# The scaling of attention's probabilities moves from GpSimd into VectorE's order

## The chip, the cores and the metric

One core of one Trainium2 chip runs the whole program, one launch of a hand-scheduled kernel: every engine has its own instruction stream, and semaphores order them. The metric is the device time of one launch in microseconds (us), the median of several runs; lower is better.

## The reference

One step of a hybrid decoder layer over 1024 prompt tokens and 8 sample tokens, all in fp32. What matters here is the prompt's attention: 8 query heads of width 64 in two groups of four (two key heads), each query block of 128 tokens attending in three branches, whose results are weighted by a gate and added:

```
s_c = einsum('nthgd,nbhd->nthgb', q, kv_cmp[:, :, 0]) * scale
p_c = masked_softmax(s_c, ...)                 # compressed: 16 blocks of keys
p_s = masked_softmax(s_s, ...)                 # selected: all keys up to the query's block
p_w = masked_softmax(s_w, w_mask)              # window of 512 keys
return gates[..., 0:1] * o_c + gates[..., 1:2] * o_s + gates[..., 2:3] * o_w
```

`masked_softmax` subtracts the row's maximum, takes the exponential and divides by the row's sum. Since the three weighted outputs are added, the kernel multiplies each head's exponentials by gate / sum (the **share**) and then adds all three products in one accumulator. Beside attention the layer has a projection of the merge gates, `h @ w_in[:, 1816:]`, 2048 columns, which doesn't depend on attention.

## The kernel before, in words

fp32 products of full accuracy are made of single-pass ones: an operand is cut into a high part (a copy rounded to the fp32r type) and a low part (the difference), and hi*hi, hi*lo and lo*hi are added.

**The attention stage** (lines 1007 to 1375) has 32 **units** (`units`, L1009), in the order i (query block, 0 to 7), kv (key head, 0 and 1), branch: first the window branch, which takes the compressed one with it (in the text "window unit"), then the selected branch ("selected unit"). A unit holds four heads, and so two **pairs**. A unit's keys are cut in **blocks** of 128 (`key_blocks`, L1018): i+1 blocks in a selected unit; min(i, 4)+1 and one of 16 compressed keys in a window unit. There are 148 blocks (`blocks`, L1027).

While the blocks of unit n are worked off, the four heads of unit n+1 are prepared: `jobs_at(t)` (L1031) says at which block t of unit n the scores of head k of unit n+1 are made. For a unit of six blocks these are blocks 0, 1, 2, 3; for units of up to three blocks all four fall on the first block.

What each engine does, in its own fixed order:

- **PE (TensorE)**, L1194 to L1204, for each block t: `scores` of the jobs (into one of two PSUM buffers; waits `exp_done` of the job two before, L1146), `turn` (L1160: four transposes of the scaled probabilities, 128 keys of four heads, into a ring of two PSUM tiles; at a unit's first block it waits until the unit's probabilities are scaled, L1165 to L1170), and `values` of the block before (L1177: products with the value rows; waits for the low part, `plo_ready`). Between these stand **fills**: steps of the merge gates' projection (`fill`, L1110; 192 steps of six products, spread over the blocks by L1046 to L1064).
- **ACT (ScalarE)**, L1249 to L1273: `exps` (exponential with bias and row sum, L1208), `cut` (the high part of a turned block, L1229), `gate` (a finished gate chunk out of PSUM, L1247), `cut_gate_hi` (the high part of the next gate weights, L918, at fixed places, L1271).
- **DVE (VectorE)**, L1354 to L1375, for each block t: `maxima` of the jobs (L1303), `cut` (the low part of the turned block, L1336), then `shares` (L1315) of a pair whose second head is done: reciprocal of the sums (L1325) times the gates (L1326). The shares of a job of block t-1 stand behind the cut of block t; those of the last block stand behind that same block's cut (L1367 to L1370). `cut_q` (L1339) and `take` (L1347) come in once per query block and once per key head.
- **POOL (GpSimd)**, L1280 to L1297: for each unit and pair, it waits for the pair's share and multiplies the exponentials of both heads, in place, by their shares (`tensor_scalar`, L1290): in a window unit 16 compressed and up to 640 window columns per head, in a selected unit (i+1)*128. For i of 5 and more, DVE takes the first head of a selected pair itself (`dve_heads`, L1014; L1327 to L1330). After the pairs of unit n come the low parts of the gate weights (`cut_gate_lo`, L920 to L923) that belong to the blocks of unit n-1. The PE's first fill on a set of gate weights waits for that low part (L1115). Fourteen of the sixteen sets are cut in this stage.
- **SP** writes the gate chunks to DRAM and loads the next gate weights (L1098 to L1106).

The stage ends with a barrier; the decode stage behind it begins with loads that SP issues after the barrier.

Of the kernel before, what the change touches and what calls it, by code (L numbers as in the profile page):

```python
# [18 lines left out]
ALU = mybir.AluOpType  # L19
AX = mybir.AxisListType  # L20

P = 128
# [11 lines left out]
WB = WINDOW // P  # L34
# [4 lines left out]
NCB = TP // BLOCK  # L39
# [37 lines left out]
class Buffers:  # L77
# [12 lines left out]
    def at(self, name, shape, dt, offset):  # L90
        size = 2 if dt == BF16 else 4
        for n in shape[1:]:
            size *= n
        assert self.base + offset + size <= self.end, (name, self.base + offset + size - self.end)
        return self.nc.alloc_sbuf_tensor_at(name, shape, dt, offset=self.base + offset), offset + (size + 31) // 32 * 32
# [148 lines left out]
def hybrid_step(nc, x_prompt, x_sample, cache_cmp_kv, cache_sel_kv, state_win_kv, state_pool, page_table,  # L244
# [3 lines left out]
    with ExitStack() as root:  # L248
        sem = Semaphores(nc)
# [34 lines left out]
        with ExitStack() as st:  # L284
# [28 lines left out]
            with nc.Block() as block:  # L313

                @block.sync
                def _(sp):
                    sp.dma_start(crow[0:1, :], c_prompt).then_inc(c_loaded, 16)
                    sp.dma_start(crow[1:1 + NS, :], c_sample).then_inc(c_loaded, 16)
                    for at_row, v in ((VB_ADA, b_ada), (VG_PRE_MIX, g_pre_mix), (VG_POST_MIX, g_post_mix),
                                      (VG_PRE_MLP, g_pre_mlp), (VG_POST_MLP, g_post_mlp), (V_POOL, pool_scale)):  # L320
                        v = v[0].rearrange("(r p) -> r p", p=P)
                        sp.dma_start(vrow[at_row:at_row + v.shape[0], :], v).then_inc(vec_loaded, 16)
                    for c in range(NA):
                        if c >= NR:
                            sp.wait_ge(ada_done, c - NR + 1)
                        sp.dma_start(wa[:, c % NR], columns_of(w_ada[0], c * AC, AC)).then_inc(wa_loaded[c % NR], 16)
                    in_load(sp)
# [170 lines left out]
        with ExitStack() as st:  # L498
            accs = [psum(st, f"in_acc{s}", [P, NCH, 512]) for s in range(2)]
            g = gin  # L500
# [161 lines left out]
        def rows_of(kv):  # L662
            return slice(kv * HD, (kv + 1) * HD)
# [232 lines left out]
        NGT = 2 * KD  # L896
# [23 lines left out]
        def cut_gate_lo(pool, u):  # L920

            pool.wait_ge(gw_hi_ready, u + 1)
            pool.tensor_tensor(gw_lo[:, u % 2], gw_raw[:, u % 2], gw_hi[:, u % 2].bitcast(F32), ALU.subtract).then_inc(gw_lo_ready, 1)  # L923
# [83 lines left out]
        SEL, WIN, CMP = 0, TP, TP + WINDOW + P  # L1007
        NKP = CMP + NCB + 2
        units = [(i, kv, br) for i in range(NB) for kv in range(KVH) for br in range(2)]  # L1009
        NUN = len(units)  # L1010
        PAIRS = GRP // 2
        RING = 2

        def dve_heads(i):  # L1014

            return 1 if i >= 5 else 0

        def key_blocks(n):  # L1018

            i, _, sel = units[n]  # L1020
            if sel:
                return [(0, b, SEL + b * P, P) for b in range(i + 1)]
            first = max(0, i - WB)
            return [(1, b, WIN + (b - first) * P, P) for b in range(first, i + 1)] + [(2, 0, CMP, NCB)]

        blocks_before = [sum(len(key_blocks(m)) for m in range(n)) for n in range(NUN + 1)]
        blocks = [(n, z) for n in range(NUN) for z in range(len(key_blocks(n)))]  # L1027
        NBL = len(blocks)
# [8 lines left out]
        def last_block(t):  # L1037

            return t + 1 == blocks_before[blocks[t][0] + 1]

        def by_dve_before(n):

            return sum(PAIRS for m in range(n) if units[m][2] and dve_heads(units[m][0]))


        NSTEP = 4 * NGU  # L1046
        FIRST = 8
# [18 lines left out]
        def gate_cuts_at(t):  # L1066

            return [x // 12 + 1 for x in steps_at[t] if x % 12 == 5 and 2 <= x // 12 + 1 < NGT]

        with ExitStack() as st:  # L1070
            at = buf.slabs(3)
            prob = at("prob", [P, GRP, NKP])
# [10 lines left out]
            share = buf.const("share", [P, 2, GRP, 3])  # L1083
# [2 lines left out]
            out = psum(st, "attn_out", [P, 512])  # L1086
            gps = psum(st, "gate_ps", [P, 512])
            qhi_ready, qlo_ready, scores_done, bias_ready, exp_done = (sem(n) for n in ("qhi_ready", "qlo_ready", "scores_done", "bias_ready", "exp_done"))
            share_ready, win_scaled, rest_scaled, sel_scaled, pT_done, phi_ready, plo_ready, pv_done, out_taken = (
                sem(n) for n in ("share_ready", "win_scaled", "rest_scaled", "sel_scaled", "pT_done", "phi_ready", "plo_ready", "pv_done", "out_taken"))  # L1090
            half_ready, zeroed_q = sem("out_half_ready"), sem("q_lo_zeroed")
            achain = sem("dve_chain3")

# [1 line left out]
            with nc.Block() as block:  # L1095
# [13 lines left out]
                def _(pe):  # L1109
# [50 lines left out]
                    def turn(t):  # L1160

                        n, z = blocks[t]
                        i, _, sel = units[n]
                        _, _, c, m = key_blocks(n)[z]
                        if z == 0 and not sel:  # L1165
                            pe.wait_ge(win_scaled, (n // 2 + 1) * PAIRS)
                        elif z == 0:
                            pe.wait_ge(rest_scaled, (n // 2 + 1) * PAIRS)
                            if dve_heads(i):
                                pe.wait_ge(sel_scaled, by_dve_before(n + 1))  # L1170
                        if t >= RING:
                            pe.wait_ge(plo_ready, t - RING + 1)
                        for g in range(GRP):
                            last = pe.transpose(pT[t % RING][0:m, g * P:(g + 1) * P], prob[:, g, c:c + m], ident[:])  # L1174
                        last.then_inc(pT_done, 1)
# [99 lines left out]
                @block.gpsimd  # L1275
                def _(pool):
                    for kv in range(KVH):
                        last = pool.memset(ql[rows_of(1 - kv), kv].bitcast(F32), 0.0)
                    last.then_inc(zeroed_q, 1)
                    for n in range(NUN):  # L1280
                        i, _, sel = units[n]
                        nw = (min(i, WB) + 1) * P
                        for pair in range(PAIRS):
                            pool.wait_ge(share_ready, n * PAIRS + pair + 1)
                            todo = [(1, SEL, (i + 1) * P)] if sel else [(2, WIN, nw), (0, CMP, NCB)]
                            own = dve_heads(i) if sel else 0
                            for g in range(2 * pair + own, 2 * pair + 2):
                                for which, c, m in todo:
                                    y = prob[:, g, c:c + m]
                                    last = pool.tensor_scalar(y, y, share[:, n // 2 % 2, g, which:which + 1], None, ALU.mult)  # L1290
                            last.then_inc(rest_scaled if sel else win_scaled, 1)
                        for t in range(blocks_before[n - 1] if n else 0, blocks_before[n] if n else 0):
                            for u in gate_cuts_at(t):
                                cut_gate_lo(pool, u)
                    for t in range(blocks_before[NUN - 1], NBL):
                        for u in gate_cuts_at(t):
                            cut_gate_lo(pool, u)  # L1297

                @block.vector
                def _(dve):  # L1300
# [14 lines left out]
                    def shares(n, pair):  # L1315

                        i, kv, sel = units[n]
                        dve.wait_ge(exp_done, n * GRP + 2 * pair + 2)
                        g0 = 2 * pair
                        g = slice(g0, g0 + 2)  # L1320
                        which = slice(1, 2) if sel else slice(0, 3, 2)
                        par = n // 2 % 2
                        x = share[:, par, g, which]
                        gates = gtok[:, i].rearrange("p (k g b) -> p k g b", k=KVH, g=GRP)[:, kv, g, which]
                        chain.then_wait(dve.reciprocal(x, total[:, par, g, which]))  # L1325
                        dve.tensor_tensor(x, x, gates, ALU.mult).then_inc(share_ready, 1)  # L1326
                        if sel and dve_heads(i):  # L1327
                            dve.wait_ge(share_ready, n * PAIRS + pair + 1)
                            y = prob[:, g0, SEL:SEL + (i + 1) * P]
                            dve.tensor_scalar(y, y, share[:, par, g0, 1:2], None, ALU.mult).then_inc(sel_scaled, 1)  # L1330

                    def cut(t):
                        n, z = blocks[t]
# [22 lines left out]
                    for k in range(GRP):  # L1356
                        maxima(0, k)
                        if k == 3:
                            shares(0, 0)
                    shares(0, 1)  # L1360
                    for t in range(NBL):
                        for n, k in jobs_at(t):
# [8 lines left out]
                        for n, k in jobs_at(t):  # L1371
                            i, kv, sel = units[n]
# [174 lines left out]
        with ExitStack() as st:  # L1547
            accs = [psum(st, f"merge_acc{s}", [P, NCH, 512]) for s in range(2)]
            g = gm
# [986 lines left out]
```

## Time and profile before

| | us |
|---|---|
| median of 3 runs | 1989.32 (1988.67 to 1989.78) |
| the profiled execution | 1988.15 |
| its span, first to last instruction | 1986.4 |
| the attention stage in it | about 416 to 934 |
| PE busy, share of the span | 89% |
| DVE, ACT, POOL busy, share of the span | 33%, 30%, 33% |

The profile is of one execution. Times in it are counted from the span's start; the 1.75 us between span and device time lie around the span. An engine's busy time is the sum of its instructions' durations; "idle before" is the time in which an engine stood still ahead of an instruction, with the work whose end released it. [...] In a row of the windows view, the busy times stand in the order PE, PEld (weight loads), DVE, ACT, POOL.

### The profile page before, as it was taken

To read this page: it belongs to the slowest core of one execution; us is meant where nothing else is said; L and a number is where in the kernel's file an instruction comes from. 1 tells how busy PE (TensorE), PEld (TensorE's weight loads), DVE (VectorE), ACT (ScalarE), POOL (GpSimd) and SP (SyncE) were. 2 spreads that over 40 slices of the span, in tenths; PEclk is the share of its full clock that TensorE was granted. 3 is DMA by queue.
4 is the path that set the end of the run, shared out by engine and by line. 5 is a ranking of instruction groups with operands and counts; after the bars stand their busy time and mean duration, and the time that the engine had idled before them with its cause. 6 is when DMAs were issued, how large, how long until landed. Compare 5 with 4: busy or idle time off the path is not lost. (4 is left out here: it accounts for less than half of the span.)

```text
span 1986.4 us, 26123 instructions
## 1 busy us (share of the span) xinstructions
PE 1773.0 (89%) x10956; PEld 1639.5 (83%) x10956; DVE 649.6 (33%) x1174; ACT 593.7 (30%) x1083; POOL 647.8 (33%) x451
## 2 busy tenths in 40 slices
PE   6899976668889888897699989899999999999997
PEld 2799965557777777775599989899999999999996
DVE  2411114243445554553144546310121121012135
ACT  3322211034445554553043435320121022002311
POOL 1454531024445553542013456222122112212421
PEclk9899996879999998998699999999999999999998
DMA  8343415301110100001264213211111111111411
GB/s 277 85 126 97 128 49 165 90 25 43 47 36 29 36 26 22 26 22 49 62 196 133 64 43 108 54 54 43 48 49 44 43 54 44 43 46 50 128 62 57
DMA packets 215048, 139.28 MB, mean 70 GB/s; under 512 B 53397, under 2 KB 211265, under 8 KB 214889
## 3 DMA queue, kind: packets, MB, share of 16 engines
q1 hardware_dynamic: 200171, 124.14, 21.8%
q10 hardware_dynamic: 14758, 13.44, 2.1%
q8 instruction: 89, 1.46, 0.3%
q14 instruction: 30, 0.25, 0.0%
HBM read 117.95 MB, written 21.92 MB: 70 GB/s over the span
## 5 line engine op out<-in xcount | busy, mean ns | idle before, releaser
L2032 POOL TENSOR_TENSOR ff_lo<-ff_raw,ff_hi 128x1024 fp32r<-128x1024 f32 x56 | 137.0, 2449 | 485.5 <-ACT ff_hi L1848 485.5
L1290 POOL TENSOR_SCALAR prob<-prob,share 128x16 f32<-128x16 f32 (+8 forms) x180 | 199.0, 1124 | 267.8 <-DVE share L1326 267.7
L1120 PE MATMUL gate_ps<-h_hi,gate_w_hi 128*128 128x344 f32 x384 | 142.9, 372 | 15.5 <-ACT gate_sum L1247 8.2
L2209 PE MATMUL ff_acc<-h_hi,ff_hi 128*128 128x344 f32 x672 | 142.6, 321 | 0.6 <-DVE relu_c L2358 0.6
L2209 PE MATMUL ff_acc<-h_lo,ff_hi 128*128 128x344 f32 x672 | 142.6, 320 | 0.0
L1336 DVE TENSOR_TENSOR p_lo<-pT,p_hi 128x512 fp32r<-128x512 f32 (+1 forms) x148 | 101.9, 688 | 122.6 <-ACT p_hi L1229 121.7
L2209 PE MATMUL ff_acc<-h_hi,ff_lo 128*128 128x344 f32 x672 | 141.9, 319 | 0.0
L1229 ACT ACTIVATE p_hi<-pT 128x512 fp32r<-128x512 f32 (+1 forms) x148 | 88.3, 597 | 164.8 <-PE pT L1174 164.3
L172 POOL TENSOR_TENSOR w_lo<-w_raw,w_hi 128x512 fp32r<-128x512 f32 (+1 forms) x31 | 56.3, 1820 | 233.1 <-ACT w_hi L168 143.8
L1218 ACT ACTIVATE prob<-scores,bias 128x640 f32<-128x640 f32 (+7 forms) x192 | 105.8, 557 | 78.8 <-DVE bias L1312 47.4
L1120 PE MATMUL gate_ps<-h_lo,gate_w_hi 128*128 128x344 f32 x384 | 127.0, 331 | 0.0
L1120 PE MATMUL gate_ps<-h_hi,gate_w_lo 128*128 128x344 f32 x384 | 126.8, 330 | 0.0
L2209 PE MATMUL ff_acc<-f_lo,ff_hi 128*128 128x344 f32 x576 | 122.2, 320 | 3.7 <-issue 3.7
L1848 ACT ACTIVATE ff_hi<-ff_raw 128x1024 fp32r<-128x1024 f32 x56 | 58.6, 1051 | 222.4 <-DMA ff_raw<-in_w_ff_dram 222.4
L2209 PE MATMUL ff_acc<-f_hi,ff_hi 128*128 128x344 f32 x576 | 122.4, 321 | 2.2 <-issue 2.2
L1174 PE MATMUL pT<-ident,prob 128*128 128x128 f32 (+1 forms) x592 | 95.8, 286 | 31.1 <-POOL prob L1290 30.9
L2209 PE MATMUL ff_acc<-f_hi,ff_lo 128*128 128x344 f32 x576 | 121.6, 319 | 0.0
L2209 PEld LDWEIGHTS ff_acc<-h_lo,ff_hi 128*128 128x128 f32 x672 | 113.7, 189 | 0.0
L2209 PEld LDWEIGHTS ff_acc<-h_hi,ff_hi 128*128 128x128 f32 x672 | 113.1, 188 | 0.8 <-issue 0.8
L2209 PEld LDWEIGHTS ff_acc<-h_hi,ff_lo 128*128 128x128 f32 x672 | 111.9, 188 | 0.0
L1174 PEld LDWEIGHTS pT<-ident,prob 128*128 128x128 f32 (+1 forms) x592 | 68.5, 141 | 49.6 <-POOL prob L1290 34.1
L1863 ACT ACTIVATE fraw<-relu 128x1032 f32<-128x1032 f32 x28 | 29.9, 1067 | 265.9 <-DVE relu L2441 265.9
(375 smaller groups left out, 4059.2 us busy)
## 6 DMA issues: line engine op xcount, KB each, us to landing
ff_raw<-in_w_ff_dram SPq DMA_DIRECT2D x56, 512.0 KB, 3.8
wa_rest<-in_w_ada_dram SPq DMA_DIRECT2D x16, 1024.0 KB, 5.3
gate_spill<-gate_sum SPq DMA_DIRECT2D x48, 172.0 KB, 1.8
gates<-gate_spill SPq DMA_DIRECT2D x16, 516.0 KB, 5.5
wa<-in_w_ada_dram SPq DMA_DIRECT2D x8, 1024.0 KB, 9.8
gate_w_raw<-in_w_in_dram SPq DMA_DIRECT2D x16, 512.0 KB, 4.1
w_raw<-in_w_in_dram SPq DMA_DIRECT2D x30, 256.0 KB, 6.4
xt<-in_x_prompt_dram ACTq DMA_DIRECT2D x4, 1024.0 KB, 9.2
```

The source lines that it names most:

```text
L172: pool.tensor_tensor(self.w.lo[:, s, 0:k], self.w.raw[:, s, 0:k], self.w.hi[:, s, 0:k].bitcast(F32), ALU.subtract).then_inc(self.lo_ready, 1)
L1120: last = pe.matmul(gps[:, 0:CH], a[:, u % 2, k], h[:, k, c * CH:(c + 1) * CH], start=(k == 0 and n == 0), stop=(k == KD - 1 and n == 2))
L1174: last = pe.transpose(pT[t % RING][0:m, g * P:(g + 1) * P], prob[:, g, c:c + m], ident[:])
L1218: last = act.activation(prob[:, k, to:to + m], ps[:, c0:c0 + m], ACT.Exp, bias=bias[:, par, k, which:which + 1], accum_out=total[:, par, k ...
L1229: act.activation(p_hi[0:m, t % RING], pT[t % RING][0:m, :], ACT.Copy).then_inc(phi_ready, 1)
L1290: last = pool.tensor_scalar(y, y, share[:, n // 2 % 2, g, which:which + 1], None, ALU.mult)
L1336: dve.tensor_tensor(p_lo[0:m, t % RING], pT[t % RING][0:m, :], p_hi[0:m, t % RING].bitcast(F32), ALU.subtract)\
L1848: act.activation(hi, raw, ACT.Copy).then_inc(wfhi_ready, 1)
L1863: act.activation(fraw[:, t], relu[:], ACT.Square).then_inc(f_squared, 1)
L2032: pool.tensor_tensor(lo, raw, hi.bitcast(F32), ALU.subtract).then_inc(wflo_ready, 1)
L2209: last = pe.matmul(accs[s][:, c, 0:CH], w[:, z % SLOTS, k], x[:, k, c * CH:(c + 1) * CH], start=(k == 0 and n == 0), stop=(k == KD - 1 and ...
```

## The change

All scalings now stand in DVE's order, behind the share of the same pair: `shares` makes the share, waits for it, and scales both heads of the pair over all their columns. POOL keeps only the low parts of the gate weights, in a plain loop without waits for anything else than their high parts. The PE's wait at a unit's first block becomes one semaphore, counted by pairs. `dve_heads` and `by_dve_before` go.

```diff
@@ turn (PE)
-                        if z == 0 and not sel:
-                            pe.wait_ge(win_scaled, (n // 2 + 1) * PAIRS)
-                        elif z == 0:
-                            pe.wait_ge(rest_scaled, (n // 2 + 1) * PAIRS)
-                            if dve_heads(i):
-                                pe.wait_ge(sel_scaled, by_dve_before(n + 1))
+                        if z == 0:
+                            pe.wait_ge(scaled, (n + 1) * PAIRS)
@@ gpsimd
-                    for n in range(NUN):
-                        i, _, sel = units[n]
-                        nw = (min(i, WB) + 1) * P
-                        for pair in range(PAIRS):
-                            pool.wait_ge(share_ready, n * PAIRS + pair + 1)
-                            todo = [(1, SEL, (i + 1) * P)] if sel else [(2, WIN, nw), (0, CMP, NCB)]
-                            own = dve_heads(i) if sel else 0
-                            for g in range(2 * pair + own, 2 * pair + 2):
-                                for which, c, m in todo:
-                                    y = prob[:, g, c:c + m]
-                                    last = pool.tensor_scalar(y, y, share[:, n // 2 % 2, g, which:which + 1], None, ALU.mult)
-                            last.then_inc(rest_scaled if sel else win_scaled, 1)
-                        for t in range(blocks_before[n - 1] if n else 0, blocks_before[n] if n else 0):
-                            for u in gate_cuts_at(t):
-                                cut_gate_lo(pool, u)
-                    for t in range(blocks_before[NUN - 1], NBL):
-                        for u in gate_cuts_at(t):
-                            cut_gate_lo(pool, u)
+                    for u in range(2, NGT):
+                        cut_gate_lo(pool, u)
@@ shares (DVE)
                         dve.tensor_tensor(x, x, gates, ALU.mult).then_inc(share_ready, 1)
-                        if sel and dve_heads(i):
-                            dve.wait_ge(share_ready, n * PAIRS + pair + 1)
-                            y = prob[:, g0, SEL:SEL + (i + 1) * P]
-                            dve.tensor_scalar(y, y, share[:, par, g0, 1:2], None, ALU.mult).then_inc(sel_scaled, 1)
+                        dve.wait_ge(share_ready, n * PAIRS + pair + 1)
+                        todo = [(1, SEL, (i + 1) * P)] if sel else [(2, WIN, (min(i, WB) + 1) * P), (0, CMP, NCB)]
+                        for head in range(g0, g0 + 2):
+                            for b, c, m in todo:
+                                y = prob[:, head, c:c + m]
+                                last = dve.tensor_scalar(y, y, share[:, par, head, b:b + 1], None, ALU.mult)
+                        last.then_inc(scaled, 1)
```

## Rows read from the trace of the kernel before

**Rows 1.** The page's 40 slices of the span: PE's busy tenths.

```profile
PE   6899976668889888897699989899999999999997
```

**Rows 2.** Earliest piece of the chain that ended last: start us, us, what.

```profile
1090.35 0.53 ACT m_hi L1798
```

**Rows 3.** Windows view, the attention stage (416 to 934 us), sum of eleven windows.

```profile
sum 518.00, PE 456.88 PEld 385.05 DVE 246.91 ACT 249.20 POOL 232.17; mean PE 41.53 PEld 35.00 DVE 22.45 ACT 22.65 POOL 21.11
```

**Rows 4.** Waits in the stage: who waited for whom, us in total, times, longest.

```profile
DVE p_lo L1336 <- ACT p_hi L1229: 121.7, 106, 3.8
...
PE pT L1174 <- POOL prob L1290: 30.9, 18, 3.3
...
PE attn_out L1186 <- DVE p_lo L1336: 6.8, 4, 2.3
PE gate_ps L1120 <- POOL gate_w_lo L923: 6.8, 3, 4.1
...
PE scores L1126 <- ACT prob L1218: 3.8, 4, 1.1
```

**Rows 5.** The page's group of POOL's scalings, all shapes.

```profile
L1290 POOL TENSOR_SCALAR prob<-prob,share 128x16 f32<-128x16 f32 (+8 forms) x180 | 199.0, 1124 | 267.8 <-DVE share L1326 267.7
```

**Rows 6.** POOL's groups of the stage by shape: count, busy us, mean ns.

```profile
L1290 POOL TENSOR_SCALAR prob<-prob,share 128x640 f32<-128x640 f32 x40 | 75.3, 1885 | 81.9 <-DVE share L1326 81.8
L923 POOL TENSOR_TENSOR gate_w_lo<-gate_w_raw,gate_w_hi 128x1024 fp32r<-128x1024 f32 x14 | 33.2, 2369 | 0.0
...
L1290 POOL TENSOR_SCALAR prob<-prob,share 128x16 f32<-128x16 f32 x64 | 20.9, 327 | 0.0
...
L1290 POOL TENSOR_SCALAR prob<-prob,share 128x1024 f32<-128x1024 f32 x4 | 13.6, 3404 | 20.2 <-DVE share L1326 20.2
```

**Rows 7.** DVE's groups of the stage by shape.

```profile
L1312 DVE TENSOR_REDUCE bias<-scores 128x1 f32<-128x18 f32 x64 | 10.6, 166 | 0.0
...
L1330 DVE TENSOR_SCALAR prob<-prob,share 128x1024 f32<-128x1024 f32 x4 | 3.0, 753 | 0.1
...
L1330 DVE TENSOR_SCALAR prob<-prob,share 128x768 f32<-128x768 f32 x4 | 2.5, 620 | 0.1
```

**Rows 8.** Timeline: two boundaries (last share, first transposes); between, DVE behind a share.

```profile
781.73 0.16 DVE L1326 TENSOR_TENSOR share<-share,gtok 128x4 f32<-128x4 f32 x1
...
786.38 0.91 PE L1174 MATMUL pT<-ident,prob 128*128 128x128 f32 x4 [2.93 <-POOL prob L1290]
...
812.94 0.82 DVE L1311 TENSOR_REDUCE bias<-scores 128x1 f32<-128x640 f32 x1 [0.86 <-PE scores L1156]
...
912.36 0.16 DVE L1326 TENSOR_TENSOR share<-share,gtok 128x2 f32<-128x2 f32 x1
...
916.07 0.89 PE L1174 MATMUL pT<-ident,prob 128*128 128x128 f32 x4 [2.48 <-POOL prob L1290]
```

**Rows 9.** Timeline at the gate weights that PE waited for longest.

```profile
476.31 1.05 ACT L918 ACTIVATE gate_w_hi<-gate_w_raw 128x1024 fp32r<-128x1024 f32 x1
...
480.54 2.34 POOL L923 TENSOR_TENSOR gate_w_lo<-gate_w_raw,gate_w_hi 128x1024 fp32r<-128x1024 f32 x1
...
482.93 0.65 PE L1120 MATMUL gate_ps<-h_hi,gate_w_hi 128*128 128x344 f32 x1 [4.10 <-POOL gate_w_lo L923]
```

**Rows 10.** Windows view: three of seven stretches with a slower clock.

```profile
477.20:487.40 10.20, 5.29 (x26) 4.79 (x25) 1.87 (x5) 2.70 (x10) 5.68 (x7) 0.67 0.27 69
786.40:790.00 3.60, 3.60 (x13) 3.30 (x14) 0.69 (x1) 2.13 (x5) 0.00 (x0) 0.53 0.00 0
916.00:926.00 10.00, 9.93 (x43) 8.05 (x44) 2.68 (x4) 2.70 (x5) 0.02 (x1) 0.66 0.00 0
```

**Rows 11.** Windows view: the window unit with i=6, kv=1.

```profile
821.04:839.30 18.26, 14.38 (x91) 11.94 (x91) 13.08 (x23) 10.89 (x19) 6.09 (x3) 0.96 0.03 11
```

**Rows 12.** The line of DVE's copies of the queries: ns min/median/max.

```profile
L1343 DVE CAST qd<-qd x16: 420/422/716, 416.9 to 834.0; 64x512 fp32r<-64x512 f32 x16
```

**Rows 13.** Waits again, in the stretch from 640 us to the stage's end.

```profile
PE pT L1174 <- POOL prob L1290: 23.5, 13, 3.3
```

More of the change, by code:

```diff
@@ L1012, in hybrid_step @@
         RING = 2
-        def dve_heads(i):
-            return 1 if i >= 5 else 0
         def key_blocks(n):
@@ L1039, in last_block @@
             return t + 1 == blocks_before[blocks[t][0] + 1]
-        def by_dve_before(n):
-            return sum(PAIRS for m in range(n) if units[m][2] and dve_heads(units[m][0]))
         NSTEP = 4 * NGU
@@ L1088, in hybrid_step @@
             qhi_ready, qlo_ready, scores_done, bias_ready, exp_done = (sem(n) for n in ("qhi_ready", "qlo_ready", "scores_done", "bias_ready", "exp_done"))
-            share_ready, win_scaled, rest_scaled, sel_scaled, pT_done, phi_ready, plo_ready, pv_done, out_taken = (
-                sem(n) for n in ("share_ready", "win_scaled", "rest_scaled", "sel_scaled", "pT_done", "phi_ready", "plo_ready", "pv_done", "out_taken"))
+            share_ready, scaled, pT_done, phi_ready, plo_ready, pv_done, out_taken = (
+                sem(n) for n in ("share_ready", "scaled", "pT_done", "phi_ready", "plo_ready", "pv_done", "out_taken"))
             half_ready, zeroed_q = sem("out_half_ready"), sem("q_lo_zeroed")
```

## The prediction

> **What bounds the kernel now.** I read the slices first: in the tenth to eighteenth, the attention stage, PE is busy for some eight tenths, against nine or more in the half behind it [rows 1]. The chain that ended last reaches back only to 1090 us, to the barrier behind the decode stage [rows 2]; it says nothing of the stage at 416 to 934 us, but each later stage starts behind a barrier, so a microsecond taken from this stage should come off the end. In the stage itself no engine but PE is near full: PE 456.9 us of 518, DVE 246.9, ACT 249.2, POOL 232.2 [rows 3]. So PE in its fixed order sets the pace, and what can be won is its 61 us of idle time. The waits say whose they are [rows 4]: 30.9 us in 18 waits for POOL's scalings, all at first blocks of units; 6.8 us in 3 waits for the gate weights' low parts, also POOL's; 6.8 us in 4 for DVE's low part of the probabilities; 3.8 us for exponentials. The rest (gate sums, the start, issue) the change doesn't touch.
>
> **POOL's scalings go.** POOL loses 180 instructions, 199 us [rows 5]. That alone is worth nothing; what counts is how long a pair takes from its share on. For a late window pair POOL needs 2 x (1.885 + 0.327) = 4.42 us; for the last selected unit 3.40 us, beside DVE's own head [rows 6].
>
> **DVE's scalings come.** DVE already runs this very instruction: 768 columns in 0.620 us, 1024 in 0.753 [rows 7]. The line through them is 0.22 us + 0.52 ns per column, so 640 columns take 0.553 us (an estimate below its ends by 128 columns). For 16 columns no row exists: bounds are 0.166 us (DVE's 18-column reduction [rows 7]) and 0.228 by the line; I take 0.20, between them. A late window pair then costs 2 x (0.553 + 0.20) = 1.5 us against POOL's 4.4; the last selected pair 2 x 0.753 = 1.5 against 3.4. By the code's loops DVE gets 40 instructions of 640 columns, 16 each of 512, 384, 256 and 128, 4 each of 768, 896 and 1024, and 64 of 16: 22.1 + 7.8 + 6.7 + 5.7 + 4.6 + 8.2 + 12.8 = 68 us (bounds 66 to 70). DVE rises to 315 us of 518, mostly into idle time such as the 121.7 us in which it waits for ACT's high parts [rows 4].
>
> **What it does to the 18 waits.** Take the boundary at 786 us. PE arrived at 786.38 - 2.93 = 783.45. The last share ended at 781.89; 1.5 us more give 783.4 instead of POOL's 786.3, so the wait just goes. At 916 us PE arrived at 913.59, the share ended at 912.52, the scalings would end at 914.0: 0.5 us of 2.48 stay [rows 8]. Working the other sixteen the same way, from their share and transposes, leaves margins of 0.02 to 2.9 us. But now pair 0's scaling stands ahead of the next maximum, and with it ahead of the last head's exponentials and pair 1's share. In a late unit DVE idles some 0.9 us ahead of that maximum while a window pair is prepared (0.86 at 812.94 [rows 8]), and hardly at all for a selected one, so that of 1.5 us, or of the 0.7 that a selected pair adds, some 0.6 are left, and the last share comes that much later. At seven late boundaries the margin is smaller than that; I put 4 us back. **Term: -30.9 + 4 = -27.** Bounds: -31 (no delay) and -16 (a full pair, 1.5 us, late at ten boundaries).
>
> **The gate weights' low parts.** POOL now does one as soon as ACT's high part is there. At the longest wait: high part ended 477.36, plus 2.34 is 479.7; PE wanted it at 482.93 - 4.10 = 478.83, so 0.9 of 4.10 stays [rows 9]. The other two waits (2.7 us) go: their high parts ended more than the 2.37 us of a cut [rows 6] before PE came. **Term: -5.9.**
>
> **What is queued behind the scalings.** Behind each pair stand, on DVE, the next maxima and the next low part; for them wait ACT's exponentials and PE's `values`. Against what DVE did next in the trace, the last pair's end pushes that work by at most 1.3 us, and `values` of a block comes a whole `turn` and its fills after the cut. So the push costs nothing where fills stand between, and its full size where PE already waits: the 4 waits for low parts (each behind a DVE copy of the queries; some 0.9 us each, 3.5 us), the one exponential at 478 us (1.2 us). In the densest unit DVE has 13.1 us in 18.3, and 1.4 more now, while PE without its waits would need 14.4 [rows 11]; four such units, half a microsecond each. **Term: +7.** Bounds: 0, if all is hidden, and +20, a third of the 68 us. The 52 added waits of DVE for its own share cost under 0.1 us each (DVE's present ones show 0.1 us of idle before the scalings in all, per shape [rows 7]) and lie in the pair prices.
>
> **The clock.** [...] Seven stretches follow waits for POOL alone. Time lost in one is (1 - clock) x PE busy: 0.33 x 5.29 = 1.7 us in the first, 0.47 x 3.60 = 1.7 in the fifth, 0.34 x 9.93 = 3.4 in the last [rows 10], 12.7 us in all seven. The last keeps a wait, so I count 9 back. **Term: -9**, bounds 0 and -13. Three more stretches follow waits for DVE's low parts and stay.
>
> **Sum.** -27 - 6 + 7 - 9 = -35. From the profiled execution's 1988.15 us that is 1953; its own time stands 1.2 us under the median of the runs, so I say **1954 us**. With the bounds at their ends: -50 (1938) and, with the unlucky end of each of the first, the third and the clock, -2; all at once is unlikely, and two together give about -16 (1973).
>
> **Rivals.**
>
> *A POOL cut holds DVE.* DVE's copies of the queries take 0.42 us, but up to 0.72 where a POOL scaling was running [rows 12]; and POOL's 1024 columns, beside a DVE scaling, took 3.40 us where its own line (327 ns at 16, 1885 at 640) gives 2.84 [rows 6]. So the two do stop each other. After the change a gate cut of 2.37 us runs right behind ACT's high part, and put behind the trace's own high parts, ten of the fourteen cuts would overlap a scaling (the one at 477.4 us [rows 9] is an early one). At up to 0.3 us each this is nothing. If instead DVE were held to the end of the cut, it would lose some 16 us there, 1.6 each, of which the margins hide most outside the late units: 6 to 10 us on PE, **1962 us**. [...] The copy that started under two POOL scalings of 2.9 us in all and lost only 0.3 speaks against it. Chance 0.10.
>
> *The wait changes its name in the late units.* If the delays through maxima and exponentials are whole pairs there, the 13 boundaries from 640 us on, 23.5 of the 30.9 us [rows 13], keep their wait, now for DVE, and the clock stays low. Left are -7.4 - 5.9 + 5 - 2, about -10: **1979 us**. For it: the small margins. Against it: 1.5 us is well below 4.4. Chance 0.11.
>
> *DVE becomes the bound, slower.* DVE works in order; if its 68 us land not in its idle time but between each low part and the next maxima with PE behind them, at 148 blocks, they go on the path. The gain without clock is 37 us, so it decides from 54% of the 68 us on; at 70% it gives 1989 - 37 + 48 = **2000 us**. Against it: DVE idles over half of the stage [rows 3]. Chance 0.07.
>
> **How the numbers follow.** Forecast 0.72, rivals 0.10, 0.11, 0.07. About 0.2% (4 us) is what a measurement can tell from no change here. The forecast, the held DVE and nearly all of the third case are faster: 0.91; 0.03 within; 0.06 slower. The range 1938 to 1974 takes in the forecast's bounds and the first rival, and leaves out the last two.
>
> **What would show it.** Right: no waits for POOL's scalings; waits of PE's transposes for DVE below 5 us; gate-weight waits near 1 us; DVE busy near 315 us in the stage; low-part waits 8 to 12 us; the stage some 35 us shorter, the later stages unchanged; a 640-column scaling near 0.55 us. Wrong: DVE scalings stretched to over a microsecond beside POOL's cuts, transposes that wait 10 us or more for DVE, or slow-clock stretches in the same places.

## The result, and the profile after

The changed kernel takes 1958.07 us (median of 4 runs, 1955.44 to 1960.03) against 1989.26; the ratio is 0.9842, with a 95% interval of 0.9825 to 0.9860. Predicted were 1954 us and a range of 1938 to 1974. The profiled execution took 1957.45 us, 30.7 less than that of before. All of it comes from the attention stage: its last VectorE (DVE) instruction ended at 935.6 us before and ends at 904.5 now.

Two windows, one of each kernel, from the stage's start to that end (columns as in [rows 11]; the figure behind POOL's busy time is the granted clock, the share of its full speed that the profile says PE was granted):

```profile
416.00:935.60 519.60, 457.13 (x2776) 385.05 (x2776) 247.59 (x528) 249.79 (x627) 232.17 (x196) 0.94 0.11 31
```

```profile
416.00:904.50 488.50, 448.24 (x2776) 377.99 (x2776) 313.04 (x708) 249.64 (x626) 34.29 (x15) 0.96 0.12 33
```

The 31.1 us split in two. TensorE (PE) is busy 8.9 us less with the same 2776 records, at a granted clock of 0.96 instead of 0.94; its idle time went from 62.5 to 40.3 us. DVE has 313 us in the stage; 315 were predicted, but the two agree by luck, as the part on the prediction shows.

Whose the idle time is now, from the waits in the stage (the answer to [rows 4]); first two waits of the kernel before that stand in no row so far, then the changed kernel:

```profile
PE gate_ps L1120 <- ACT gate_sum L1247: 8.2, 14, 1.1
...
PE attn_out L1186 <- DVE qT L1351: 0.7, 2, 0.4
```

```profile
PE gate_ps L1111 <- ACT gate_sum L1234: 12.6, 18, 1.9
PE scores L1117 <- ACT prob L1205: 12.1, 6, 3.5
PE attn_out L1173 <- DVE p_lo L1310: 7.8, 5, 2.6
...
PE pT L1161 <- DVE prob L1303: 1.6, 3, 1.0
PE attn_out L1173 <- DVE qT L1325: 1.5, 4, 0.7
```

The 30.9 us of waits for POOL's scalings have become 1.6 us for DVE's, and the 6.8 us for gate weights are gone altogether. But the wait for exponentials has grown from 3.8 to 12.1 us, and that for gate sums (ACT empties a finished gate chunk) from 8.2 to 12.6. The groups of DVE by shape point to a reason:

```profile
L1303 DVE TENSOR_SCALAR prob<-prob,share 128x640 f32<-128x640 f32 x40 | 21.7, 551 | 0.7
L1303 DVE TENSOR_SCALAR prob<-prob,share 128x16 f32<-128x16 f32 x64 | 16.7, 261 | 0.0
...
L1297 DVE TENSOR_TENSOR share<-share,gtok 128x2 f32<-128x2 f32 x32 | 9.6, 300 | 1.1
L1303 DVE TENSOR_SCALAR prob<-prob,share 128x512 f32<-128x512 f32 x16 | 9.6, 619 | 0.3
```

640 columns cost 0.551 us, as estimated (0.553). But 512 columns cost more than 640, and the little product that makes the shares, untouched by the change, takes 0.300 us on average in its two-column form; in the kernel before all 64 of both forms took 0.162 to 0.195. The timeline shows single instructions that are far too long, nine in the stage, each beside a POOL cut of gate weights (the instruction that makes their low part). Two places:

```profile
451.99 2.41 POOL L923 TENSOR_TENSOR gate_w_lo<-gate_w_raw,gate_w_hi 128x1024 fp32r<-128x1024 f32 x1 [35.94 <-ACT gate_w_hi L918]
452.08 0.17 DVE L1296 RECIPROCAL share<-total 128x4 f32<-128x4 f32 x1
452.28 2.15 DVE L1297 TENSOR_TENSOR share<-share,gtok 128x4 f32<-128x4 f32 x1
...
478.45 2.98 DVE L1303 TENSOR_SCALAR prob<-prob,share 128x256 f32<-128x256 f32 x4
478.97 2.43 POOL L923 TENSOR_TENSOR gate_w_lo<-gate_w_raw,gate_w_hi 128x1024 fp32r<-128x1024 f32 x1 [24.57 <-ACT gate_w_hi L918]
...
482.47 0.58 PE L1117 MATMUL scores<-k_st,qd 128*128 128x256 f32 x1 [3.48 <-ACT prob L1205]
```

POOL's cut ends at 454.40, DVE's share at 454.43; POOL's second cut ends at 481.40, DVE's four scalings, 0.90 us where no cut runs, at 481.43. Such an overlap that lengthens a DVE instruction is called a **meeting** below. Behind the four scalings stand the maxima, behind these the exponentials, and PE waits 3.48 us at 482.47.

### The profile page after: what moved, and what is told of

Read it like the earlier page. It is cut to its first block and busy times, and to the rows that moved or that the text cites. A ratio compares the mean times of both kernels' runs of the same rounds, so it can differ in the third digit from the quotient of the medians.

```text
span 1955.7 us, 26123 instructions
## 1 busy us (share of the span) xinstructions
PE 1760.1 (90%) x10956; PEld 1630.7 (83%) x10956; DVE 715.2 (37%) x1354; ACT 594.0 (30%) x1083; POOL 451.1 (23%) x271
## 3 DMA queue, kind: packets, MB, share of 16 engines
q1 hardware_dynamic: 200171, 124.14, 22.1%
## 5 line engine op out<-in xcount | busy, mean ns | idle before, releaser
L1111 PE MATMUL gate_ps<-h_hi,gate_w_hi 128*128 128x344 f32 x384 | 141.2, 368 | 13.0 <-ACT gate_sum L1234 12.6
L923 POOL TENSOR_TENSOR gate_w_lo<-gate_w_raw,gate_w_hi 128x1024 fp32r<-128x1024 f32 x16 | 40.5, 2534 | 481.0 <-ACT gate_w_hi L918 481.0
L2415 DVE TENSOR_SCALAR relu<-ff_acc 128x1032 f32<-128x1032 f32 x28 | 34.5, 1233 | 200.1 <-PE ff_acc L2183 200.1
L2183 PEld LDWEIGHTS ff_acc<-f_lo,ff_hi 128*128 128x128 f32 x576 | 97.5, 189 | 4.1 <-issue 4.1
```

The costliest lines, as they stand in the source:

```text
L1111: last = pe.matmul(gps[:, 0:CH], a[:, u % 2, k], h[:, k, c * CH:(c + 1) * CH], start=(k == 0 and n == 0), stop=(k == KD - 1 and n == 2))
L2183: last = pe.matmul(accs[s][:, c, 0:CH], w[:, z % SLOTS, k], x[:, k, c * CH:(c + 1) * CH], start=(k == 0 and n == 0), stop=(k == KD - 1 and ...
L2415: dve.tensor_scalar(by_chunk(relu[:]), out(m % 2), 0.0, None, ALU.max).then_inc(ff_taken[m % 2], 1)
```

## The experiments

Two theories stand against each other. **Holding**: POOL's cut, while in flight, holds DVE's scalings and shares, and that is what PE now waits for; it is the prediction's first rival. **Length**: it is the scalings themselves, standing ahead of the maxima, that make the exponentials late. The first three kernels change only POOL's loop in the changed kernel; the next two take one half of the change alone; the last repeats it.

**POOL's cuts behind the scaling.** POOL does a unit's gate-weight cuts only when the next unit's pairs are scaled, which is their old place.

```diff
-                    for u in range(2, NGT):
-                        cut_gate_lo(pool, u)
+                    for n in range(NUN + 1):
+                        cuts = [u for t in range(blocks_before[n - 1] if n else 0, blocks_before[n] if n else 0) for u in gate_cuts_at(t)]
+                        if cuts and n < NUN:
+                            pool.wait_ge(scaled, (n + 1) * PAIRS)
+                        for u in cuts:
+                            cut_gate_lo(pool, u)
```

> The changed kernel, but POOL starts the gate weights' low parts of a unit's blocks only when the next unit's pairs are all scaled, as in the kernel before. Theory (the two engines exclude each other: in the changed kernel nine DVE instructions are stretched to the end of a POOL cut, some 14 us in all, and PE then waits 12.1 us for exponentials instead of 3.8): no stretched DVE instruction, the wait for exponentials back to 4 to 6 us, a new wait for gate weights of 1 to 3 us; about 5 us less than the changed kernel's 1958, so 1951 to 1955. Rival (it is the scalings' own length ahead of the maxima that makes the exponentials late): the wait for exponentials stays at 10 to 12 us, and the time is 1957 to 1961.

Measured: 1940.65 us, ratio 0.9756 (0.9737 to 0.9774), faster than both kernels: the interval lies wholly below that of the changed kernel. Its waits in the stage and its groups by shape:

```profile
PE gate_ps L1111 <- ACT gate_sum L1234: 11.2, 18, 1.9
PE attn_out L1173 <- DVE p_lo L1314: 7.8, 5, 2.6
PE scores L1117 <- DVE ql L1322: 5.1, 1, 5.1
PE scores L1117 <- ACT prob L1205: 4.4, 4, 1.4
PE attn_out L1173 <- DVE qT L1329: 1.5, 4, 0.7
PE gate_ps L1111 <- POOL gate_w_lo L923: 0.9, 1, 0.9
PE pT L1161 <- DVE prob L1307: 0.4, 1, 0.4
```

```profile
L1307 DVE TENSOR_SCALAR prob<-prob,share 128x16 f32<-128x16 f32 x64 | 14.6, 228 | 0.0
L1307 DVE TENSOR_SCALAR prob<-prob,share 128x512 f32<-128x512 f32 x16 | 7.4, 484 | 0.3
...
L1301 DVE TENSOR_TENSOR share<-share,gtok 128x4 f32<-128x4 f32 x32 | 5.3, 165 | 1.1
```

No stretched instruction is left, and the wait for exponentials is back at 4.4 us with the scalings in the same place: length falls. The gain over the changed kernel, 17 us, is more than three times what was expected. Where it comes from, the window of the stage tells:

```profile
416.00:888.40 472.40, 441.49 (x2776) 372.84 (x2776) 299.73 (x708) 250.07 (x626) 33.35 (x15) 0.97 0.12 34
```

The stage is 16.1 us shorter than in the changed kernel; PE is busy 6.8 us less at a clock of 0.97, and idle 9.4 us less, of which 7.7 are the wait for exponentials. So the meetings cost DVE 13.3 us (313.0 against 299.7) and PE 9.4 us of standing still. The further 6.8 us go with the clock; some of that comes and goes between executions, since the repeat of the changed kernel at the end of this part has PE busy 2.4 us less.

**Quarter cuts.** Each cut in four POOL instructions of 256 columns, at the changed kernel's place.

```diff
-                        cut_gate_lo(pool, u)
+                        pool.wait_ge(gw_hi_ready, u + 1)
+                        for k in range(0, KD, 2):
+                            last = pool.tensor_tensor(gw_lo[:, u % 2, k:k + 2], gw_raw[:, u % 2, k:k + 2],
+                                                      gw_hi[:, u % 2, k:k + 2].bitcast(F32), ALU.subtract)
+                        last.then_inc(gw_lo_ready, 1)
```

> The changed kernel, with each gate-weight cut of POOL made in four instructions of 256 columns. [...] Rival (DVE is held for as long as POOL has work, or the stretch is not what PE waits for): nothing changes, 1957 to 1961.

On holding, if a hold ends with the POOL instruction in flight, the author's estimate was 5 to 8 us of waits for exponentials and a time of 1951 to 1956 us.

Measured: 1950.66 us, ratio 0.9804 (0.9790 to 0.9818), an interval just below that of the changed kernel; PE waits 8.5 us for exponentials, a little above the 5 to 8 expected. The line of the share product, ns min/median/max, here, and its longest case beside POOL's four quarters:

```profile
L1301 DVE TENSOR_TENSOR share<-share,gtok x64: 162/164/560, 430.7 to 877.0; 128x4 f32<-128x4 f32 x32, 128x2 f32<-128x2 f32 x32
```

```profile
452.74 2.79 POOL L1270 TENSOR_TENSOR gate_w_lo<-gate_w_raw,gate_w_hi 128x256 fp32r<-128x256 f32 x4 [35.47 <-ACT gate_w_hi L918]
...
453.61 0.56 DVE L1301 TENSOR_TENSOR share<-share,gtok 128x4 f32<-128x4 f32 x1
```

Its worst case is 0.56 us instead of 2.15, and it ends at 454.17, where the third of the four quarters has just begun (at 454.12); the four run on to 455.53. So this share was held to the end of one POOL instruction, and did not wait for the two behind it.

**Double cuts.** A second POOL instruction over the same 1024 columns, times one, behind each cut.

```diff
-                        cut_gate_lo(pool, u)
+                        pool.wait_ge(gw_hi_ready, u + 1)
+                        pool.tensor_tensor(gw_lo[:, u % 2], gw_raw[:, u % 2], gw_hi[:, u % 2].bitcast(F32), ALU.subtract).then_inc(gw_twice, 1)
+                        pool.wait_ge(gw_twice, u - 1)
+                        pool.tensor_scalar(gw_lo[:, u % 2], gw_lo[:, u % 2].bitcast(F32), 1.0, None, ALU.mult).then_inc(gw_lo_ready, 1)
```

> The changed kernel, with a second POOL instruction over the same 1024 columns behind each gate-weight cut (times one), so that POOL has twice the work or more at each of the 14 places. Theory (POOL's instruction holds DVE): the holds on DVE grow from 14 us to 25 to 35, the wait for exponentials to 18 to 25 us, and the time to 1966 to 1975. Rival (POOL's work there costs PE nothing): 1957 to 1961, apart from gate weights that come 2.5 us later, at most 2 us.

Measured: 1972.79 us, ratio 0.9917 (0.9902 to 0.9932). The waits in the stage:

```profile
PE scores L1118 <- ACT prob L1206: 15.6, 6, 3.5
...
PE pT L1162 <- DVE prob L1307: 4.7, 4, 2.6
```

The time is as expected, the way to it only in part: the wait for exponentials grew to 15.6 us and not to 18 to 25, and DVE is busy 321.4 us in the stage, 21.7 more than without meetings, where 25 to 35 were expected. The last part shows that the added instruction holds DVE less than the cut does (0.87 us at the most against some 2). Still, POOL work that PE itself waits for only 0.9 us costs 15 us: of the changed kernel's waits, those for exponentials grew by 3.5 us, those of the transposes for DVE by 3.1.

**The window units' half alone.** The kernel before, with DVE scaling the window units' pairs; POOL keeps its part of the selected units, and its cuts stand behind a unit's scalings.

```diff
+                        if not sel:
+                            pool.wait_ge(win_scaled, (n // 2 + 1) * PAIRS)
-                        for pair in range(PAIRS):
+                        for pair in range(PAIRS if sel else 0):
...
@@ shares (DVE)
+                        if not sel:
+                            dve.wait_ge(share_ready, n * PAIRS + pair + 1)
+                            for head in range(g0, g0 + 2):
+                                for b, c, m in [(2, WIN, (min(i, WB) + 1) * P), (0, CMP, NCB)]:
+                                    y = prob[:, head, c:c + m]
+                                    last = dve.tensor_scalar(y, y, share[:, par, head, b:b + 1], None, ALU.mult)
+                            last.then_inc(win_scaled, 1)
```

> The kernel before, with the window units' scalings alone moved to DVE; POOL keeps its part of the selected units' and cuts the gate weights where it did. In the profile of before the waits at window units are 22 of 30.9 us. If the gain comes boundary by boundary, as the prediction has it, this kernel takes about 22 us of waits, 3 of gate weights and some 5 of clock, gives 3 back, and stands at 1960 to 1966. If instead the gain hangs on POOL being free altogether (the DVE and POOL instructions meeting), it stands at 1970 or more.

Measured: 1950.73 us, ratio 0.9810 (0.9795 to 0.9825), better than the 1960 to 1966 expected and, in its median, than the whole change. PE's remaining waits for POOL:

```profile
PE pT L1174 <- POOL prob L1288: 8.8, 7, 2.5
...
PE gate_ps L1120 <- POOL gate_w_lo L923: 0.9, 1, 0.9
```

Of 30.9 us, 22.1 went: as many as stood at window units. The cuts got earlier too, with POOL ahead of them free: the second starts at 477.95 instead of 480.54 us, with the high part ready at 477.4 in both. No DVE instruction is stretched beside a cut here. What the expectation had too small is the clock, with 5 us; the windows behind the next kernel show 14.

**The selected units' half alone.** The mirror image: DVE scales the selected units wholly, POOL the window units, cuts behind a unit's scalings.

```diff
-                        for pair in range(PAIRS):
+                        if sel:
+                            pool.wait_ge(rest_scaled, (n // 2 + 1) * PAIRS)
+                        for pair in range(0 if sel else PAIRS):
...
@@ shares (DVE)
-                        if sel and dve_heads(i):
+                        if sel:
                             dve.wait_ge(share_ready, n * PAIRS + pair + 1)
-                            y = prob[:, g0, SEL:SEL + (i + 1) * P]
-                            dve.tensor_scalar(y, y, share[:, par, g0, 1:2], None, ALU.mult).then_inc(sel_scaled, 1)
+                            for head in range(g0, g0 + 2):
+                                y = prob[:, head, SEL:SEL + (i + 1) * P]
+                                last = dve.tensor_scalar(y, y, share[:, par, head, 1:2], None, ALU.mult)
+                            last.then_inc(rest_scaled, 1)
```

> The kernel before, with the selected units' scalings alone wholly on DVE; POOL keeps the window units' and cuts the gate weights where it did, behind a unit's scalings. The window half alone gave 38 us, both halves without meetings (POOL's cuts behind the scaling) 48. If the boundaries add up, this half gives about 10 us: 1976 to 1982, with PE waiting some 20 us for POOL at window units. If the halves need each other (a wait that goes at one boundary only turns up at the next), it gives under 4 us: 1985 or more.

Measured: ratio 0.9911 (0.9894 to 0.9927), 1974.41 us against 1992.00 in its own series: 17.6 us, more than the 10 expected. The waits:

```profile
PE pT L1172 <- POOL prob L1288: 22.2, 11, 3.3
...
PE gate_ps L1120 <- POOL gate_w_lo L923: 7.0, 3, 4.2
```

The two halves' waits for POOL's scalings add up (22.1 + 8.7 = 30.8 of 30.9); their times don't: 38 + 18 against 48 for both without meetings. The stage's windows of the two halves say where the excess lies:

```profile
416.00:897.20 481.20, 443.17 (x2776) 373.68 (x2776) 280.14 (x656) 250.97 (x627) 119.57 (x68) 0.97 0.12 34
```

```profile
416.00:919.50 503.50, 445.53 (x2776) 375.92 (x2776) 267.26 (x580) 251.44 (x628) 147.43 (x144) 0.96 0.11 32
```

PE's idle time falls by 24.4 and 4.5 us, about the 31.6 of both together; its busy time by 14.0 and 11.6, far more than the 15.6 of both. So the excess is the clock's: what one kernel gets back from it is no sum over the boundaries.

**The change once more.**

> The changed kernel itself, once more beside the kernel before, to see how far two series of it agree: 1955 to 1961. The stretched DVE instructions should stand at the same gate-weight cuts if they are a matter of the two engines' order, and at others if of chance.

Measured: 1962.14 us against 1992.00, ratio 0.9848 (0.9832 to 0.9865), a little above the expected 1955 to 1961, but the kernel before is slower in this series too. The stage itself is not longer than in the first series:

```profile
416.00:903.20 487.20, 445.81 (x2776) 375.58 (x2776) 313.12 (x708) 250.53 (x627) 35.28 (x16) 0.96 0.12 33
```

The wait for exponentials is again 12.1 us in 6 waits, and the four scalings beside the second cut take 2.98 us again, at 478.68; at the first cut it is once more the second share that is held, 2.14 us at 453.72. All nine stretched instructions stand at the same cuts as in the first series. The meetings belong to the order of the two engines and not to chance.

## Why the prediction was right, and where it was not

The sum was right (35 us predicted, 31 measured), but in part by luck: without meetings the change gains 46.6 us by the terms below, 11.6 more than predicted, and the meetings, which the forecast put at nothing, take 16 of them back. The two errors are each larger than the difference that is left.

| term, us | predicted | changed kernel | cuts behind scaling |
|---|---|---|---|
| transposes' waits | -27 | -29.3 | -30.5 |
| gate weights | -5.9 | -6.8 | -5.9 |
| work pushed behind the scalings | +7 | +14.5 | +5.4 |
| clock | -9 | -8.9 | -15.6 |
| sum | -35 | -30.5 | -46.6 |

The third line adds the growth of four waits of PE: exponentials, low parts, gate sums and the output's sum; in the changed kernel 8.3 + 1.0 + 4.4 + 0.8. The fourth is PE's busy time, at the same 2776 records. The rest up to the 31.1 us of the stage is its earlier start.

- **The 18 waits** went as worked out; the two halves agree with the list by kind of unit. The 4 us put back for late shares were too much: 1.6 with meetings, 0.4 without.
- **DVE's prices** held for single instructions: 0.551 us at 640 columns. For 16 columns the line's end of the bounds was right (0.228 us without meetings), not the middle. What the sums of prices left out is that in these traces one such instruction begins some 0.09 us before the recorded end of the one ahead of it. A late window pair takes 1.30 us, where 2 x (0.551 + 0.228) are 1.56, and not 1.5 (in the kernel with the cuts behind the scaling):

```profile
783.50 1.30 DVE L1307 TENSOR_SCALAR prob<-prob,share 128x640 f32<-128x640 f32 x4
```

- **DVE's busy time** met its forecast by luck. A window's busy time counts such overlaps once, and is not the plain sum of durations. The 68 us were added to it as a sum; without meetings it rose by 52.1 us (299.73 against 247.59), and the meetings' 13.3 bring it to 313.
- **The step that failed** is the one that put the meetings at nothing: "At up to 0.3 us each this is nothing". The forecast took a meeting's price from DVE's copies beside POOL's scalings [rows 12]. Beside POOL's cuts, DVE's shares and scalings were held to the end (a share for 2.15 us instead of 0.165): ten overlaps and some 16 us were the rival's own working, and DVE lost 13.3. So the rival with chance 0.10 is what happened, and the prediction's own sign of being wrong, DVE scalings stretched to over a microsecond beside POOL's cuts, was there. The rival's price on PE, 6 to 10 us, was the standing still alone (9.4 us); with the clock the stage loses 16.1 us, or 14.8 by the repeat.
- **Work pushed**: without meetings +5.4 for the 7 predicted, though more of it in gate sums (+3.0) and less at the low parts (+1.0) than placed there. In the changed kernel, with the meetings, it is 14.5.
- **The clock** gave 8.9 for 9, but again by an offset: without meetings 15.6 come back, above the bound of 13. The step that failed here is that three stretches behind waits for DVE's low parts "stay". Two of them, in the kernel before, and the same two places with the cuts behind the scaling, where the waits for the low parts are still there:

```profile
761.80:773.00 11.20, 10.58 (x41) 8.34 (x42) 4.27 (x10) 2.73 (x7) 4.96 (x2) 0.54 0.00 0
835.90:849.00 13.10, 11.49 (x51) 8.52 (x52) 4.86 (x11) 3.71 (x11) 5.35 (x2) 0.61 0.04 13
```

```profile
737.50:748.70 11.20, 11.20 (x65) 9.21 (x66) 6.45 (x14) 4.78 (x13) 2.36 (x1) 0.85 0.09 20
802.60:815.70 13.10, 13.06 (x79) 10.93 (x80) 9.33 (x23) 5.90 (x18) 2.35 (x1) 0.87 0.04 15
```

  The granted clock rose from 0.54 and 0.61 to 0.85 and 0.87, and PE works off half as many matmul records again in the same time. In the changed kernel the second place still has 0.61:

```profile
815.40:828.50 13.10, 12.83 (x56) 9.86 (x57) 7.36 (x13) 4.26 (x13) 1.49 (x1) 0.61 0.04 13
```

  There a share is held by a cut (1.41 us at 815.50); whether that keeps the clock low was not tested. Nor does a run show that a slow stretch comes from the wait ahead of it and goes with it; this was the author's estimate, and the -9 us rests on it. Before, these two places had 0.54 and 0.61 behind waits for low parts of 2.1 and 2.3 us, and with the cuts behind the scaling 0.85 and 0.87 behind waits of 2.6 us each. [rows 10] and the windows here give the clock of a stretch, not its cause.
- **The range** rests in part on a slip: two unlucky ends of the bounds together give -11 to -15 us (1974 to 1978), not "about -16 (1973)". The measured time is far from there.
- **The other rivals.** The waits did not change their name in the late units (1.6 us in 3 waits for DVE in the whole stage), and DVE at 313 of 488 us did not become the bound.

## What to carry to other kernels

When work moves off an engine, look at what the engine still does, and when: freed of its old queue, POOL's remaining 2.4 us instruction came earlier and fell on the very instructions that had been moved. Price a meeting of two engines by a row with the same pair of instructions; here a row of another kind from the same engine was no bound on it (0.3 us beside POOL's scalings, up to 2.18 beside its cuts). The recorded durations of DVE instructions that follow one another closely overlapped here, by some 0.09 us each: don't add their sum to a busy time of a window. An order that looks like a needless wait may be what keeps two engines apart, and putting that wait back (1941 us) was worth 17 us, more than half of what the change itself won (31).

## What the runs showed of the hardware that was not expected

In these runs it depends on POOL's instruction whether a share beside it is held. In the kernel before, 15 of the 64 shares were made while POOL scaled, at no cost; of that kernel's trace, a POOL scaling of eight instructions in flight and a share beside it, and then the line of all shares:

```profile
431.01 3.55 POOL L1290 TENSOR_SCALAR prob<-prob,share 128x128 f32<-128x128 f32 x8 [14.44 <-DVE share L1326]
...
431.50 0.17 DVE L1326 TENSOR_TENSOR share<-share,gtok 128x4 f32<-128x4 f32 x1
```

```profile
L1326 DVE TENSOR_TENSOR share<-share,gtok x64: 162/165/195, 430.7 to 912.4; 128x4 f32<-128x4 f32 x32, 128x2 f32<-128x2 f32 x32
```

The same product beside POOL's subtraction of two tensors took up to 2.15 us in the changed kernel. The two POOL instructions differ in the number of tensors that they read, one against two, and in length. The double cuts tell these apart, since their second instruction reads one tensor and is the longer one:

```profile
453.32 2.40 POOL L1270 TENSOR_TENSOR gate_w_lo<-gate_w_raw,gate_w_hi 128x1024 fp32r<-128x1024 f32 x1 [35.93 <-ACT gate_w_hi L918]
...
453.60 2.14 DVE L1301 TENSOR_TENSOR share<-share,gtok 128x4 f32<-128x4 f32 x1
...
751.24 3.19 POOL L1272 TENSOR_SCALAR gate_w_lo<-gate_w_lo 128x1024 fp32r<-128x1024 f32 x1
...
752.18 0.16 DVE L1301 TENSOR_TENSOR share<-share,gtok 128x2 f32<-128x2 f32 x1
752.38 1.15 DVE L1307 TENSOR_SCALAR prob<-prob,share 128x768 f32<-128x768 f32 x2
```

Beside the subtraction the share is held to its end once more. Beside the longer instruction a share takes 0.16 us and two scalings of 768 columns 1.15, twice 0.618 less the overlap. So length is not what makes the difference between the two. The one-tensor instruction is not free of cost either: at other places of that run single DVE scalings beside it took up to 0.87 us longer, and in the kernel before a copy of the queries beside POOL's scalings took 0.72 us instead of 0.42. Whether the second tensor or the operation makes the difference, no run separates. And not every DVE instruction beside a cut was held: the reciprocal took 0.17 us, and the low parts, which read one operand from PSUM, never more than 0.694, in the changed kernel as before:

```profile
L1310 DVE TENSOR_TENSOR p_lo<-pT,p_hi x148: 671/690/694, 435.7 to 901.6; 128x512 fp32r<-128x512 f32 x132, 16x512 fp32r<-16x512 f32 x16
```
